# A hybrid encoder trunk in fp32: at seven entries GpSimd makes the first 1024 columns of one weight unit's low part, between the two roots of the norm

## The reference, cut to what matters

```python
def reference(x, ...):
    alpha = (2.0 * DEPTH) ** 0.25
    for i in range(DEPTH):
        ...
        x = layer_norm(alpha * x + h, ln_mix_g[i], ln_mix_b[i])
        x = layer_norm(alpha * x + sq_relu_mlp(x, ffn_w_in[i], ffn_w_out[i]),
                       ln_ffn_g[i], ln_ffn_b[i])
    return x

def layer_norm(x, g, b):
    xf = x.astype(jnp.float32)
    mu = jnp.mean(xf, axis=-1, keepdims=True)
    var = jnp.mean(jnp.square(xf - mu), axis=-1, keepdims=True)
    y = (xf - mu) * lax.rsqrt(var + EPS)
    return y.astype(x.dtype) * g + b
```

## Time and profile before

| | before |
|---|---|
| executions | 1495.07, 1498.05, 1498.57 us (median 1498.05) |
| profiled execution | 1495.12 us, of which the span of the program is 1493.2 us |
| TensorE, matmuls | busy 1431.4 us (96%) |
| VectorE | busy 999.0 us (67%) |
| ScalarE | busy 770.6 us (52%) |
| GpSimd | busy 199.0 us (13%) |
| share of the chain that ended last | PE 75%, DVE 11%, ACT 4%, issue 3% |

### The profile page before, as it was taken

The page is one execution under the profiler, slowest core; times in us unless marked ns, Lnnn a source line. Parts: engine busy times, 40 slices in busy tenths (PEclk is TensorE's granted clock), DMA queues, the critical chain, the costliest instruction groups (busy, mean ns, idle before and its releaser), DMA issues.

```text
span 1493.2 us, 24585 instructions
## 1 busy us (share of the span) xinstructions
PE 1431.4 (96%) x9723; PEld 1323.8 (89%) x9723; DVE 999.0 (67%) x1229; ACT 770.6 (52%) x1105; POOL 199.0 (13%) x245
## 2 busy tenths in 40 slices
PE   7899998999999999999999999999999999999996
PEld 7888997999989989998899889998998899799995
DVE  5889898554577575455644465455798899855554
ACT  4776775444424334444355535442487787454441
POOL 2222221622210000000000000000032221200000
PEclk9999999999999999999999999999999999999998
DMA  8666554667656454645543245655656564555550
GB/s 243 201 196 225 170 170 141 181 189 228 191 185 220 158 198 159 213 170 199 195 158 126 85 141 174 220 173 175 188 180 212 185 185 154 169 178 189 198 197 29
DMA packets 198192, 266.96 MB, mean 179 GB/s; under 512 B 11768, under 2 KB 167824, under 8 KB 198080
## 3 DMA queue, kind: packets, MB, share of 16 engines
q1 hardware_dynamic: 188720, 237.72, 48.3%
q0 software_dynamic: 9200, 27.55, 5.8%
q10 hardware_dynamic: 160, 0.13, 0.0%
HBM read 264.19 MB, written 1.18 MB: 178 GB/s over the span
## 4 chain that ended last, share of the span: by engine, by line
PE 75%; DVE 11%; ACT 4%; issue 3%; POOL 0%; DVEq 0%; ACTq 0%
PE acc L587 33%; PE y L739 28%; PE acc L608 8%; DVE w_low L1519 3%; DVE conv L1655 3%; ACT w_high L1113 1%; PE y L608 1%; PE inner L897 1%; PE inner L709 1%; ACT E L1223 1%; ACT xT L1143 1%; DVE x_tokens L1570 1%; DVE x_tokens L1564 0%; DVE E L1685 0%; DVE stats L1557 0%
## 5 line engine op out<-in xcount | busy, mean ns | idle before, releaser
L587 PE MATMUL acc<-xT,w_high 128*128 128x256 f32 x3264 | 595.9, 284 | 5.4 <-DVE w_low L1519 5.4
L1519 DVE TENSOR_TENSOR w_low<-raw,w_high 128x2048 fp32r<-128x2048 f32 (+1 forms) x226 | 513.7, 2283 | 89.2 <-ACT w_high L1113 61.4
L1113 ACT ACTIVATE w_high<-raw 128x2048 fp32r<-128x2048 f32 (+1 forms) x226 | 427.2, 1896 | 192.4 <-DMA raw<-in_ffn_w_in 74.2
L587 PEld LDWEIGHTS acc<-xT,w_high 128*128 128x128 f32 x3264 | 512.5, 192 | 10.8 <-issue 7.1
L587 PE MATMUL acc<-xT,w_low 128*128 128x256 f32 x1632 | 462.3, 283 | 0.0
L739 PE MATMUL y<-w_high,opT 128*128 128x512 f32 x1408 | 397.1, 391 | 0.2 <-DVE opT L1942 0.2
L587 PEld LDWEIGHTS acc<-xT,w_low 128*128 128x128 f32 x1632 | 313.5, 192 | 0.0
L739 PEld LDWEIGHTS y<-w_high,opT 128*128 128x128 f32 x1408 | 259.6, 188 | 51.2 <-issue 1.0
L739 PE MATMUL y<-w_low,opT 128*128 128x512 f32 x704 | 222.7, 390 | 0.0
L1538 DVE TENSOR_TENSOR opT<-conv,opT 128x512 fp32r<-128x512 f32 x56 | 38.9, 694 | 264.5 <-issue 236.6
L608 PE MATMUL acc<-w_high,xT 128*128 128x256 f32 (+1 forms) x928 | 182.0, 298 | 9.6 <-DVE xT L1583 8.6
(11 more groups left out here) (221 smaller groups left out, 1206.3 us busy)
## 6 DMA issues: line engine op xcount, KB each, us to landing
raw<-in_ffn_w_in SPq DMA_DIRECT2D x128, 512.0 KB, 4.7
raw<-in_ffn_w_out SPq DMA_DIRECT2D x128, 512.0 KB, 4.4
raw<-in_ssd_w_in SPq DMA_DIRECT2D x96, 512.0 KB, 5.2
E<-cumsum_dram POOLq DMA_DIRECT2D x32, 512.0 KB, 6.0
raw<-in_ssd_w_out SPq DMA_DIRECT2D x32, 512.0 KB, 4.5
raw<-in_sc_w_in SPq DMA_DIRECT2D x24, 512.0 KB, 4.8
raw<-in_na_w_qkv SPq DMA_DIRECT2D x24, 512.0 KB, 4.6
raw<-in_sc_w_out SPq DMA_DIRECT2D x8, 512.0 KB, 4.7
```

Of the source, the lines that this page charges most:

```text
L587: mm = nc.tensor.matmul(bank[:, c * SEQ:(c + 1) * SEQ][:, span], w[:, col:col + P], xT[:, k, low, span], start=(k == 0 and part == 0), sto ...
L1113: nc.scalar.activation(w_high[:, u % SPLIT, c0:k * c], raw[:, u % RAW, c0:k * c], ACT.Copy).then_inc(w_high_done, 1)
L1519: V.tensor_tensor(w_low[:, u % SPLIT, c0:k * c], raw[:, u % RAW, c0:k * c], f(w_high[:, u % SPLIT, c0:k * c]), ALU.subtract).then_inc(w_lo ...
```

## The change

One unit at each of the seven entries is shared: `fi` 2 in the four MLPs, `ch` 0, `v` 0, and `z` 1 in the second SSD. DVE makes only its columns 1024 to 2047. GpSimd makes columns 0 to 1023 with one TENSOR_TENSOR, which stands between the root of t = 0 and the root of t = 1, and counts it on a new semaphore. PE (where it takes the unit) and SP (where it loads over the unit's raw slot) wait for that one too.

```diff
+        pool_low = sem("pool_low")
...
+        shared_unit = {}
+        for s, (kind, _, names) in enumerate(subs):
+            if s:
+                shared_unit[s] = names[{"ffn": ("fi", HEAD_UNITS - 1), "ssd": ("z", 1), "conv": ("ch", 0), "attn": ("v", 0)}[kind]]
+        shared = sorted(shared_unit.values())
+
+        def pool_half_done(engine, u):
+
+            if u in shared:
+                engine.wait_ge(pool_low, shared.index(u) + 1)
...
                     sp.wait_ge(w_low_done, u - RAW + 1)
+                    pool_half_done(sp, u - RAW)
...
                 for t in range(NT):
+                    if t and s + 1 in shared_unit:
+                        low_half(shared_unit[s + 1])
                     pool.wait_ge(var_done, 2 * s + t + 1)
...
+            def low_half(u):
+
+                pool.wait_ge(w_high_done, u + 1)
+                pool.wait_ge(w_used, u - SPLIT + 1)
+                pool.wait_ge(raw_landed[u % RAW], 32 * (u // RAW + 1))
+                nc.gpsimd.tensor_tensor(w_low[:, u % SPLIT, 0:UNIT // 2], raw[:, u % RAW, 0:UNIT // 2],
+                                        f(w_high[:, u % SPLIT, 0:UNIT // 2]), ALU.subtract).then_inc(pool_low, 1)
...
                 pe.wait_ge(w_low_done, u + 1)
+                pool_half_done(pe, u)
...
+                    if u in shared:
+                        c0 = UNIT // 2
                     dve.wait_ge(w_high_done, u + 1)
```

## The result

The changed kernel takes **1507.37 us** (median of five executions, 1504.55 to 1512.01) beside 1498.05 us for the kernel before in the same comparison (five executions, 1495.07 to 1499.95). The ratio is 1.0065 with an interval of [1.0052, 1.0078]: 7.8 to 11.7 us slower, 9.3 by the medians. The forecast was 1498.8 with a range up to 1503.5; the time lies outside. The profiled execution took 1507.21 us, its span 1505.5, so it stands close to its median, whereas the one of before lay 2.9 us under its own. Differences between the two profiles therefore come out larger than 9.3 us, and I use them for single places, not for the sum.

What follows compares the result with a forecast made beforehand. TensorE was taken to bound the kernel, busy 96% of the span, with 3.78 us of waits for the second norm. Gains and losses at the entries summed to +0.75 us on the median 1498.05, giving 1498.8 us; range 1494.0 to 1503.5.

Steps and rivals of the forecast that it cites:

- Who goes first: At the seven entries: VectorE first where ACT releases both engines, its half 1.07 us sooner; GpSimd first at two boundaries.
- the sum: Over the entries: gains 0.23, 0.97 and 0.23 us, losses 1.09 us at second MLP and second SSD; +0.75 us in all.
- The exclusion: At the shared halves: one engine waits for the other's whole two-operand instruction; GpSimd's hold for 1024 columns 2.21 us.
- VectorE's half: At each of the seven entries: 1.22 us for 128x1024 instead of 2.29, so 1.07 us less.
- The boundary in the second MLP and second SSD: Between two low parts of VectorE there: GpSimd goes first, VectorE's half lasts 3.37 us, the norm comes 1.09 us later.
- Attention and third MLP worth nothing: At these two entries: no gain, as PE had no wait at the third MLP and attention's half is not ahead of a norm.
- The rest at nothing: At the entries: second root, SP's load, gain and bias DMAs and PE's extra waits cost nothing, except where said.
- The convolution's: At the convolution's turn: PE waits 0.53 us for GpSimd's half of the unit, leaving a gain of 0.97 us.
- the prediction's two side sums: The sum over the entries with other holds: 0.08 us higher with 2.25 us, about 0 with 1.82 us.
- The clock: TensorE after the turns: 1.28 us for a 1.2 GHz stretch; less idle at convolution, more at second MLP, taken to cancel.
- GpSimd goes first everywhere: Rival, where ACT releases both engines: VectorE loses 1.09 us at each of five entries, +5.45 us, 1503.5 us; chance 0.13.
- a rival of its own (1501.4): Rival, TensorE behind two turns: idle grows 1.1 us each, two further 1.2 GHz stretches cost 2.6 us; chance 0.10.

Runs made afterwards that it cites:

- the version with VectorE first: The changed kernel, with GpSimd's half made to wait until VectorE's half of the unit is done; 1495.70 us, 0.9975 of the kernel before.
- the two costly parts of the change: The change at second MLP and second SSD alone, 1503.92 us; at first MLP, convolution and last MLP alone, 1504.33 us; 1.0030 and 1.0037 of the kernel before.

## Why the prediction was wrong

**The step that failed** is "*Who goes first*", in its first point: "while GpSimd has two more waits to pass and 0.13 us of start. I take it that VectorE goes first". In its place the trace has GpSimd first at all five entries where ACT releases both, by 0.01 us (0.02 at the third MLP), and VectorE's half takes 3.44 to 3.47 us there instead of 1.22. For the first MLP, the convolution and the last MLP together the sum had -1.43 us; TensorE's waits show +3.29. The two further waits cost no time that the trace shows. And the 0.13 us of start was my own reading of what GpSimd's 1.04 us contains; it didn't put GpSimd behind VectorE. The engines' rows begin together, and I had given a probability of 0.13 to what a lead of 0.01 us decides. The trace of before held no case where one event releases both; I named that, and still weighed it as if the number of waits told the order.

Point by point:

- *The exclusion*, "one waits for the other's whole instruction": right. The size too: hold forecast 2.21 us, measured 2.26.
- *VectorE's half*: 1.22 us forecast, 1.22 to 1.23 wherever GpSimd doesn't go first.
- *The boundary in the second MLP and second SSD*: right, 3.37 us forecast, 3.42 in the row above; waits of 1.9 and 2.1 us forecast before the turns, 1.90 and 1.91 found. For the two entries together the sum had 2.18 us, and the waits grew by 1.99.
- *Attention and third MLP worth nothing*: right, 1.0003 [0.9992, 1.0014].
- *The rest at nothing* (the second root, SP's load, the two DMAs, the waits): right; with the same waits and queues the version with VectorE first gains.
- *The convolution's* 0.53 us wait at `ch` 0: 0.59 where GpSimd's half starts just behind VectorE's, as the sum had it. It is 0.81 where GpSimd waits for VectorE's count and so starts later. Right. But the prediction's two side sums leave this wait out: with a hold of 2.25 us the sum would be 0.12 us higher, not 0.08, and with 1.82 it would be -0.13.
- *The clock*, "I let the two cancel": mis-sized. It was put at nothing and costs up to 3.5 us of the 9.3 (up to 5.1 by the largest mean of the kernel before). In the two costly parts of the change, and where VectorE alone made the delay, the mean granted clock also lay below that of the kernel before.
- *The rival "GpSimd goes first everywhere"*: the right mechanism at +5.45 us, with the clock left out of it; 5.28 us of idle time is what the rows show. The clock stood as a rival of its own (1501.4), as if only one of the two could come true. Taken together they would have given 5.45 + 2.6 = 8.1 us and 1506.1. The range ended at 1503.5, this rival's value without the clock.

Left open is why a stretch at 1.2 GHz comes at one entry and not at another. In the profile of after there is one behind the turns in the second SSD and last MLP, and none in the 14 us behind the first MLP's turn, after the same wait of 1.40 us, nor in those behind the second MLP's, after 1.90 us. I have granted clocks, not their cause.

## What to carry to other kernels

When work is handed from VectorE to GpSimd and both read SBUF, the first question is not how long the instruction takes but who starts first. If one event releases both, treat the order as unknown and price both cases, or fix it: make GpSimd wait for VectorE's own count, so that it runs beside steps of VectorE with at most one SBUF operand. And price a delay on the path at more than its length: here 1.2 us of delay before a turn cost about 1.9 us (1.6 to 2.3, the change's interval over five), and TensorE's idle time was in part followed by stretches at half its clock.

## What was unexpected of the hardware

- A lead of 0.01 us decides for 2.26 us. Where one event releases both, GpSimd went first in 5 of 5 entries with a lead of 0.01 to 0.02 us, and VectorE in 5 of 5 when GpSimd's row began 0.02 to 0.03 us behind.
- GpSimd's two-operand subtraction of 1024 columns takes 2.38 to 2.40 us undisturbed, VectorE's 1.22; a write of the same columns on GpSimd takes 0.95 and doesn't hold VectorE up.
- A delay of 1.26 us, made by VectorE alone, at five entries that matter cost 11.0 us (9.0 to 13.2): 2.2 us each, nearly twice its length.
